# HGRN's last products issued together, two heads per product in MLA and banded attention, and a division one pair behind

## What is computed

```
for l in range(2):
    h = rmsnorm(x)
    a_cq, a_ckv, a_kr, b_q, b_ff, b_fb, b_i, b_g, c_q, c_k, c_v, gates = split(h @ w_in[l])
    y_a = mla(...)      # 8 heads: softmax(q k^T / sqrt(96)) v, q and k of width 96, v of width 64, 512 x 512 scores
    y_b = hgrn2(...)    # ... o = rmsnorm(o_f + o_b, g_out) * silu(g)
    y_c = window(...)   # 8 heads of width 64 that share k and v by fours; blocks of 128 queries see
                        # 3 blocks of keys (2 at the ends); p = exp(s - m) / (sum exp(s - m) + exp(sink - m)),
                        # m = max(max s, sink), s = q k^T / 8 + bias
    x = x + (sum of sigmoid(gate) * (y @ w_br)) @ w_out
    x = x + cross(...);  x = x + swiglu(...)
```

## Time and profile before

| | |
|---|---|
| median of three runs | 4083.86 us |
| profiled execution, its own time / its span | 4075.39 / 4073.2 us |
| busy: PE / DVE / ACT / POOL | 93% / 48% / 37% / 19% |
| mean granted clock of TensorE, in shares of full speed | 0.957 |
| chain that ended last: PE / DVE / ACT / issue / POOL | 75% / 10% / 6% / 5% / 3% |
| MLA's heads, layer 0 and layer 1 (first exponential to last transpose) | 1441.5 to 1511, 2795.9 to 2866 us |
| banded attention, layer 0 and layer 1 (first `ws` to last `ych`) | 1832.9 to 1894.9, 3187.9 to 3251.7 us |

### The profile page before, as it was taken

How to read it: one execution, slowest core, us unless ns; L and a number is a source line. 1 busy time by engine, 2 the same in 40 slices (tenths; PEclk the granted TensorE clock), 3 DMA queues, 4 the chain that set the end, 5 groups by cost and what they waited for, 6 DMA issues and landing times.

```text
span 4073.2 us, 60895 instructions
## 1 busy us (share of the span) xinstructions
PE 3790.8 (93%) x25654; PEld 3075.0 (75%) x25654; DVE 1935.7 (48%) x3078; ACT 1510.6 (37%) x2533; POOL 770.0 (19%) x790
## 2 busy tenths in 40 slices
PE   6889998999999999988999999998999799999998
PEld 3568887887888747776888788875677688777886
DVE  5556555535444565635334533336465533444333
ACT  3433233323323345734223332224575422343222
POOL 0122122221211123432111110102244211101010
PEclk8999999989999899999999999998999899999999
DMA  5321010012222202111223122220111022222222
GB/s 183 125 84 18 3 52 13 3 53 104 99 96 96 68 16 72 59 58 37 97 95 119 59 97 99 97 79 26 62 63 63 16 96 96 88 102 84 98 94 87
DMA packets 81111, 300.87 MB, mean 74 GB/s; under 512 B 8776, under 2 KB 9928, under 8 KB 79944
## 3 DMA queue, kind: packets, MB, share of 16 engines
q1 hardware_dynamic: 80840, 296.99, 21.5%
HBM read 292.76 MB, written 4.19 MB: 73 GB/s over the span
## 4 chain that ended last, share of the span: by engine, by line
PE 75%; DVE 10%; ACT 6%; issue 5%; POOL 3%; DMA 1%; DVEq 0%; SPq 0%; POOLq 0%; ACTq 0%
PE ps L205 74%; PE ps L210 1%; DVE wlo L236 1%; DVE he L244 1%; ACT whi L224 1%; DVE hc L2334 1%; DVE tmp L244 1%; ACT ha L224 1%; DVE ac L244 1%; ACT wp L225 1%; DVE ha L236 1%; ACT L224 1%; DVE ss L244 1%; DVE q L236 1%; DMA wraw<-weights 0%
## 5 line engine op out<-in xcount | busy, mean ns | idle before, releaser
L236 DVE TENSOR_TENSOR wlo<-wraw,whi 128x1024 fp32r<-128x1024 f32 x537 | 682.1, 1275 | 771.6 <-ACT whi L224 770.9
L205 PE MATMUL ps<-hh,whi 128*128 128x512 f32 x1840 | 733.4, 399 | 19.1 <-DVE hl L236 13.9
L205 PE MATMUL ps<-hl,whi 128*128 128x512 f32 x1840 | 723.8, 393 | 0.0
L205 PE MATMUL ps<-hh,wlo 128*128 128x512 f32 x1840 | 723.5, 393 | 0.0
L224 ACT ACTIVATE whi<-wraw 128x1024 fp32r<-128x1024 f32 x537 | 559.8, 1050 | 223.1 <-PE ps L205 169.6
L205 PEld LDWEIGHTS ps<-hh,whi 128*128 128x128 f32 x1840 | 349.8, 190 | 103.7 <-ACT hh L224 20.1
L205 PEld LDWEIGHTS ps<-hh,wlo 128*128 128x128 f32 x1840 | 350.1, 190 | 74.7
L205 PEld LDWEIGHTS ps<-hl,whi 128*128 128x128 f32 x1840 | 350.7, 191 | 70.7
L205 PE MATMUL ps<-u,u 64*64 64x64 f32 (+2 forms) x6016 | 229.0, 228 | 25.6 <-DVE u L236 17.0
L205 PEld LDWEIGHTS ps<-u,u 64*64 64x64 f32 (+1 forms) x6016 | 209.5, 139 | 42.3 <-DVE u L236 18.1
L205 PE MATMUL ps<-gh,whi 128*128 128x512 f32 x528 | 205.4, 389 | 0.0
(11 more groups left out here) (391 smaller groups left out, 7145.7 us busy)
## 6 DMA issues: line engine op xcount, KB each, us to landing
wraw<-weights SPq DMA_DIRECT2D x537, 512.0 KB, 3.2
x<-xT SPq DMA_DIRECT2D x2, 2048.0 KB, 12.4
bias_lines<-ln SPq DMA_DIRECT2D x1, 2048.0 KB
xmf<-memT SPq DMA_DIRECT2D x2, 1024.0 KB, 4.7
out<-x SPq DMA_DIRECT2D x1, 2048.0 KB, 6.2
bias<-bias_lines SPq DMA_DIRECT2D x1, 1536.0 KB, 8.7
con<-consts SPq DMA_DIRECT2D x1, 1378.0 KB, 10.5
ctxt<-ctxT SPq DMA_DIRECT2D x1, 1024.0 KB, 12.5
```

The costliest lines, as they stand in the source:

```text
L205: self.last, self.open = self.e.matmul(out, lhsT, rhs, start=start, stop=stop, skip_group_check=skip), True
L236: return self.e.tensor_tensor(out, a, b, op)
```

## The change

PE, ACT, DVE and POOL get other orders in the two stages; no DMA changes. In short: in MLA PV of two heads is issued after the second head's transposes, the heads in turn for each block of keys, with two buffers `ptt` in place of one, and no bank is held. In HGRN's end POOL does all four `hy` and then all four `hyl`, and ACT does `act_hgrn_out` ahead of the copy `wv`. The banded attention goes by pairs c of heads: the scores of both in turn, then the transposes of pair c-1, head by head, and O of pair c-1, the two heads in turn. DVE adds the bias of one head, divides a head of the pair before, adds the bias of the other head, divides the other one; then it takes all four maxima of a head in one reduce over 4x384 (the two unused ends of 128 are filled with -1e30 once per buffer and layer), with one small operation after it, and at the end of the turn waits for `ych`. `ws` has three buffers.

```diff
-            L.PT = self.ring(f"pt{l}", [self.sb("ptt", M + 4096, [128, 4, 512])], lambda q=qdone: [q()])
+            L.PT = self.ring(f"pt{l}", [self.sb("ptt", M + o, [128, 4, 512]) for o in (4096, 11776)], rdone)
-            L.wS = self.ring(f"ws{l}", [self.sb("ws", M + 3072 + 1536 * i, [128, 4, 384]) for i in range(2)], after_b)
+            L.wS = self.ring(f"ws{l}", [self.sb("ws", M + o, [128, 4, 384]) for o in (3072, 4608, 12288)], after_b)
@@ pe_mla
-                b = ps.take(pe, "mo", l, i // 2, hold=True) if e == 0 else ps["mo", l, i // 2 - 1]
-                q = L.PT[z]
-                for kc in range(4):
-                    hd = i - 1
-                    pe.wait_ge((K.act if kc % 2 else K.dve).at("mt", l, hd, kc), K.act.at("mv", l, 3))
-                    pe.mm(b[64 * e:64 * e + 64, :], L.V[:, kc, hd * 64:hd * 64 + 64], q[:, kc, :], kc == 0, kc == 3)
...
                 if e == 1:
+                    b = ps.take(pe, "mo", l, i // 2 - 1)
+                    for kc in range(4):
+                        pe.wait_ge([(K.act if kc % 2 else K.dve).at("mt", l, hd, kc) for hd in (i - 2, i - 1)], K.act.at("mv", l, 3))
+                        for hd in (i - 2, i - 1):
+                            r, q = slice(64 * (hd % 2), 64 * (hd % 2) + 64), L.PT["ms", l, hd]
+                            pe.mm(b[r, :], L.V[:, kc, hd * 64:hd * 64 + 64], q[:, kc, :], kc == 0, kc == 3)
...
@@ pool_hgrn_out
             pool.tt(s3, L.G4[:, i, :], s2, ALU.mult).then_inc(pool("hy", l, i), 1)
             pool.also(f"ht2{l}", l, i)
+        for i in range(4):
+            s3 = L.t3[l, i]
             pool.wait_ge(K.act.at("hyh", l, i), pool.at("hy", l, i))
             pool.tt(K.Y["b"][1][:, i, :], s3, K.Y["b"][0][:, i, :].bitcast(F32), ALU.subtract).then_inc(pool("hyl", l, i), 1)
@@ pe_window
+        for c in range(5):
+            if c < 4:
+                for n, k0, k1, w, off in K.spans():
+                    b = [ps.take(pe, "ws", l, 2 * c + e, n) for e in range(2)]
+                    pe.wait_ge(act.at("wq", l, c), act.at("wk", l))
+                    for e, r in enumerate(rows):
+                        pe.mm(b[e][:, 0:w], L.wQ[r, c, n * 128:n * 128 + 128], L.wK[r, k0 * 128:k1 * 128])
+                    pe.mark("ws", l, 2 * c + 1, n)
+                    pe.also("ws", l, 2 * c, n)
+            if c > 0:
+                for i in (2 * c - 2, 2 * c - 1):
+                    for n, k0, k1, w, off in K.spans():
+                        b = ps.take(pe, "wt", l, i, n)
+                        pe.wait_ge(K.divided(z, n))
...
+                bo = ps.take(pe, "wo", l, c - 1)
+                for n, k0, k1, w, off in K.spans():
+                    pe.wait_ge([act.at("wt", l, 2 * c - 2 + e, n) for e in range(2)], act.at("wv", l))
+                    for j in range(k1 - k0):
+                        for e, r in enumerate(rows):
+                            q = L.wT["ws", l, 2 * c - 2 + e]
+                            pe.mm(bo[r, n * 128:n * 128 + 128], L.wV[:, k0 + j, 64 * e:64 * e + 64],
+                                  q[:, n, j * 128:j * 128 + 128], j == 0, j == k1 - k0 - 1)
@@ act_window
+        K.act_hgrn_out(l)
         act.wait_ge(pe.at("wv", l))
         act.cp(L.wV.rearrange("p a b -> p (a b)"), ps["wv", l]).then_inc(act("wv", l), 1)
-        K.act_hgrn_out(l)
+        for c in range(5):
+            for i in (2 * c - 2, 2 * c - 1) if c > 0 else ():
+                q = L.wT.take(act, "ws", l, i)
+                for n, k0, k1, w, off in K.spans():
+                    act.wait_ge(pe.at("wt", l, i, n))
+                    act.cp(q[:, n, 0:w], ps["wt", l, i, n][:, 0:w]).then_inc(act("wt", l, i, n), 1)
...
+            for e in range(2) if c < 4 else ():
+                z = ("ws", l, 2 * c + e)
...
                 for n, k0, k1, w, off in K.spans():
                     K.act_exp(z, n, p[:, n, 0:w], s[:, n, 0:w], 1.0)
+                act.also(f"ws{l}", *z)
                 K.act_sink(z, 4, K.vec(f"sink{l}")[:, c + 4 * e:c + 4 * e + 1])
+            if c > 0:
+                act.wait_ge(pe.at("wo", l, c - 1))
+                act.cp(K.Y["c"][0][:, c - 1, :], ps["wo", l, c - 1]).then_inc(act("wo", l, c - 1), 1)
@@ dve_window
+        for s in L.wS.aps:
+            dve.wait_ge(K.ended("hgrn", l))
+            dve.e.memset(s[:, 0:4:3, 256:384], -1e30).then_inc(dve("wpads", l), 1)
+        for c in range(5):
+            for e in range(2):
+                if c < 4:
+                    hd, z = c + 4 * e, ("ws", l, 2 * c + e)
...
+                    for n, k0, k1, w, off in K.spans():
+                        dve.wait_ge(pe.at(*z, n))
+                        dve.stt(s[:, n, 0:w], ps[(*z, n)][:, 0:w], 0.125, ALU.mult, K.bias[:, hd, off:off + w], ALU.add).then_inc(dve("wb", *z), 1)
...
+                if c > 0:
+                    z = ("ws", l, 2 * c - 2 + e)
+                    K.dve_divide(z, [L.wP[z][:, n, 0:w] for n, _, _, w, _ in K.spans()], sink=True)
+            for e in range(2) if c < 4 else ():
+                s, sm = L.wS[z], K.sml.take(dve, *z)
+                dve.e.reduce_max(sm[:, 0:4], s, AXX).then_inc(dve("mx", *z), 1)
+                dve.ts(sm[:, 8:12], sm[:, 0:4], sink, ALU.max, -1.0, ALU.mult).then_inc(dve("ng", *z, 3), 1)
+            if c > 0:
+                dve.wait_ge(act.at("wo", l, c - 1))
+                dve.tt(yl, ps["wo", l, c - 1], yh.bitcast(F32), ALU.subtract).then_inc(dve("wo", l, c - 1), 1)
```

More of the change, by code:

```diff
@@ L2528, in pe_window @@
                 [(b[:, c * 128:c * 128 + 128], c == 0) for c in range(4)], h)
[L2529 to L2532, removed]
+        rows = [slice(64 * e, 64 * e + 64) for e in range(2)]
+        for c in range(5):
+            if c < 4:
                 for n, k0, k1, w, off in K.spans():
-                    b = ps.take(pe, *z, n)
+                    b = [ps.take(pe, "ws", l, 2 * c + e, n) for e in range(2)]
@@ new lines, in pe_window @@
+                    pe.mark("ws", l, 2 * c + 1, n)
+                    pe.also("ws", l, 2 * c, n)
+            if c > 0:
+                for i in (2 * c - 2, 2 * c - 1):
+                    z = ("ws", l, i)
+                    for n, k0, k1, w, off in K.spans():
+                        b = ps.take(pe, "wt", l, i, n)
+                        pe.wait_ge(K.divided(z, n))
+                        for j in range(k1 - k0):
+                            pe.tr(b[:, j * 128:j * 128 + 128], L.wP[z][:, n, j * 128:j * 128 + 128], K.con("id"))
+                        pe.mark("wt", l, i, n)
+                    pe.also(f"wp{l}", *z)
+                bo = ps.take(pe, "wo", l, c - 1)
@@ L2549, in pe_window @@
[L2549 to L2556, removed]
@@ L2576, in act_window @@
         act.also("ps", "wv", l)
-        K.act_hgrn_out(l)
[L2578 to L2581, removed]
-                for n, k0, k1, w, off in K.spans():
[L2583 to L2588, removed]
+        for c in range(5):
+            for i in (2 * c - 2, 2 * c - 1) if c > 0 else ():
+                q = L.wT.take(act, "ws", l, i)
+                for n, k0, k1, w, off in K.spans():
+                    act.wait_ge(pe.at("wt", l, i, n))
+                    act.cp(q[:, n, 0:w], ps["wt", l, i, n][:, 0:w]).then_inc(act("wt", l, i, n), 1)
+                    act.also("ps", "wt", l, i, n)
+            for e in range(2) if c < 4 else ():
+                z = ("ws", l, 2 * c + e)
                 s, p = L.wS[z], L.wP.take(act, *z)
@@ L2591, in act_window @@
                     K.act_exp(z, n, p[:, n, 0:w], s[:, n, 0:w], 1.0)
+                act.also(f"ws{l}", *z)
                 K.act_sink(z, 4, K.vec(f"sink{l}")[:, c + 4 * e:c + 4 * e + 1])
[L2593 to L2596, removed]
+            if c > 0:
+                act.wait_ge(pe.at("wo", l, c - 1))
+                act.cp(K.Y["c"][0][:, c - 1, :], ps["wo", l, c - 1]).then_inc(act("wo", l, c - 1), 1)
+                act.also("ps", "wo", l, c - 1)
         act.mark("end", "window", l)
@@ L2609, in dve_window @@
         K.dve_feed("wv", l)
[L2610 to L2620, removed]
-                sink = K.vec(f"sink{l}")[:, hd:hd + 1]
[L2622 to L2632, removed]
@@ new lines, in dve_window @@
+        for s in L.wS.aps:
+            dve.wait_ge(K.ended("hgrn", l))
+            dve.e.memset(s[:, 0:4:3, 256:384], -1e30).then_inc(dve("wpads", l), 1)
+        for c in range(5):
+            for e in range(2):
+                if c < 4:
+                    hd, z = c + 4 * e, ("ws", l, 2 * c + e)
+                    s = L.wS.take(dve, *z)
+                    dve.wait_ge(K.loaded("bias"))
+                    for n, k0, k1, w, off in K.spans():
+                        dve.wait_ge(pe.at(*z, n))
+                        dve.stt(s[:, n, 0:w], ps[(*z, n)][:, 0:w], 0.125, ALU.mult, K.bias[:, hd, off:off + w], ALU.add).then_inc(dve("wb", *z), 1)
+                        dve.also("ps", *z, n)
+                if c > 0:
+                    z = ("ws", l, 2 * c - 2 + e)
```

(16 more changed lines are left out.)

22 lines of the change are left out of this document (6 added, 16 removed).

## The result

The changed kernel took **4035.27 us**, median of 5 runs (4026.32 to 4047.8); the one before, 5 times in the same session, 4083.86 us (4070.18 to 4100.83). The ratio is 0.9888, 95% interval 0.9848 to 0.9927: 49 us less, where 43 were forecast. In a later session 6 runs of it gave 4046.55 us against 4085.86 (11 runs), ratio 0.9891 (0.9867 to 0.9916).

What follows compares the result with a forecast made beforehand. PE was taken to bound the whole span and MLA, no single engine the banded attention. MLA's -18 and -25 from HGRN's end with the banded attention gave -43 us: 4083.9 to 4041 us, range 4020 to 4066.

Steps and rivals of the forecast that it cites:

- PV by pairs: MLA: two heads' PV on the two column halves takes 3.6 us instead of 7.2; -9.0 us a layer, -18 in all.
- Two middle periods: MLA between head 3 and head 7: a pair takes 14.9 us instead of 17.92; -6.0 us a layer.
- The end: MLA's last head: its transposes have neither scores nor PV for cover while waiting for the division; +1.4 us a layer.
- The start: MLA's start: scores of head 2 begin without PV(0) ahead of them; -4.4 us a layer.
- HGRN's end: POOL's chain finishes ahead of the scores, so DVE's first `ws` starts at 1821.2 instead of 1832.87; -11.7 us a layer.
- Pairs of the banded attention: Turns slightly slower per pair, with DVE waiting for `ych`, yet 60.9 us in sum against 62.0; -1.1 us a layer.
- turn 0: Banded attention's first turn: sums and maxima only, paced by the scores; 7.6 us.
- turn 1: Banded attention's second turn: waits 0.3 us for the sink and meets a slow PE; 15.0 us.
- turn 4: Banded attention's last turn: POOL's division, transposes, copy, then O; 8.1 to 10.2 us, taken as 9.3.
- upper case D: Both stages gain more: POOL's wait hidden in MLA, banded turns of 12.5 us; -62 us, 4022; chance 0.15.
- B: Banded attention: PE's low clock delays transposes and copies, so a turn takes 16.5 us; +12 us, 4053; chance 0.15.
- E: MLA: waits for POOL let PE's clock fall to half; +61 us with the other gain, 4145; chance 0.05.

Runs made afterwards that it cites:

- e3: Changed kernel with a pair's PV in MLA issued one head after the other instead of in turn; MLA 71.7 / 72.3 us in the two layers.
- e2: Kernel before with only the new POOL and ACT orders at HGRN's end; banded attention 105.1 / 105.1 us, profiled run 4065.11 us.
- e9: Kernel before, unchanged, profiled a second time; 4082.24 us, first exponential of MLA at 1451.7 us.
- e5: Changed kernel with ACT copying `ych` between the two new heads' exponentials instead of behind both; banded attention 95.3 / 95.3 us.
- e6: Changed kernel with DVE's `ycl` made one turn later and the products' bank held till then; banded attention 92.8 / 93.1 us.
- e8: Changed kernel with the edits of e6 and e7 together; 4029.39 us median of 6 runs, ratio to the kernel before 0.9871.
- e7: Changed kernel with DVE dividing three of four blocks of every odd MLA head, POOL one instead of two; MLA 63.1 / 63.2 us.
- e11: Changed kernel with the edit of e6, plus DVE's third block for MLA's head 7 alone; 4006.56 us, ratio to before 0.9805.

## Why the prediction was right

**PV by pairs (-18; measured -8.4 and -9.3, -17.7).** The row of HGRN, 16 records in 1.09 us against 20 in 2.40, carried over to 512 columns: 3.65. The Trainium skill, "TensorE: Matmul & The Clock Gate", Part 3, says that a weight load overlaps a matmul in flight only on another row group. The traces contradict it, before the change too: in one head's PV a load at 1461.40 us lies inside the matmul record of 1461.29 to 1461.88 on the same 128 rows. That products on two column halves would bring next to nothing was my inference from it; the same Part lists three tiles side by side in the columns at 2.38 times, and with that these runs agree (two halves, 3.65 us for 7.2). e3 shows that the order of issue is what decides. Two middle periods gave 2 x (17.92 - 14.72) = -6.4, forecast -6.0, since POOL came 0.4 us earlier than I had worked out. The end took 10.9 us from T(6)'s end, forecast 9.3 + 1.4 = 10.7, so it cost 1.6. The start gave -3.7 in layer 0, forecast -4.4: PV(0) is gone from there, but head 2's scores now meet the lower clock in its place, 4.55 us for 3.70.

**HGRN's end (-11.7 a layer; e2: -10.5 and -12.4).** All steps of it stand in the traces: POOL's two lists, ACT's `ybh` ahead of `wv`, the scores as the new releaser. The start of `ws` moved by 12.42 - 0.83 = 11.6 against the scores. That the marks of two layers differ by 2 us belongs to one execution of before: 115.6 and 117.5, in e9 115.5 and 115.9, against which e2 gains 10.4 and 10.8.

**Pairs of the banded attention (-1.1, of which -0.8 was taken; measured -0.8 and -1.0 beyond e2).** The mechanism held: DVE waits for `ych` behind both heads' exponentials. The size did not, and the total hides it. From first `ws` to last `ych`, the mark of the forecast, it is 62.4 us in layer 0 where the sum of turns had 60.9 and before has 62.0: turn 0 7.4 (forecast 7.6), turn 1 15.6 (15.0), then 15.2 and 15.0 (14.5 each), turn 4 9.2 (9.3). Over both profiles of each kernel and both layers it is 62.1 against 62.5 before, 0.5 us less and not 1.1. The longer turns come from T's side: ACT's last `wt` ends at 1857.4, 9.0 after `ycl`'s end at 1848.4, where I had 8.1 for it. About 0.6 of that is the lower clock, 1.97 us for the second head's transposes in place of 1.41, which the forecast of the turn had at nothing. My upper case D took 12.5 for a turn "if ACT takes work before I let it"; e5 shows that it needs an edit, and e6 that 11.35 is there.

**Sum.** -42.4 by the stages, forecast -43. The 4041 us of the forecast lie 6 us over the median of the first session and 6 below that of the second; the runs of one kernel spread over 20 to 30 us, so this is as near as a median of five can tell. No rival came as a whole: PE's clock fell in the banded attention (0.72), where B expected it, and B's mechanism is there, but with some 0.6 us a turn in place of 2.0; in MLA the waits for POOL are 0.23 us and the mean over 1454 to 1520 is 0.90, with the low part at the two ends and PV and scores of the middle pairs at 3.65 and 3.70 as before, so E had nothing to decide on. That the sum came within 1 us is partly luck, since the start of MLA and the turns gave less than forecast, and the middle pairs of MLA and layer 1, long in that one profile of before, gave more.

**What was sized wrong on the way:** e3 at 79 us for 72, because I counted heads in line as wholly serial, though the earlier trace rows had already shown 16 scores in 3.60 against 8 in 2.42, the same effect; e8 at 4005 for 4029, because its base was of another session; and the pair of e7, where I took POOL's wait away and did not ask what DVE's extra block makes late.

## What to carry to other kernels

When an engine stands in line for a result whose producer has other work listed ahead of it, look for the instruction that can be taken a turn later without cost; here that one move (e6) was worth 11 us a layer, as much as the whole reordering of HGRN's end, for one bank held longer. Shift work between engines only where the receiver has slack at that very place: the same third block on DVE cost 0.4 us in a middle pair and gained 2.7 at the end. And compare stages between fixed marks before whole times, since one part that varies by 17 us from execution to execution can hide or double a gain of that size.

## What the runs showed of the hardware

Products of 64 columns of stationary operand on either half of the columns, and products of 64 rows on either half of the rows, run beside each other fully when issued in turn: 16 records of 512 columns in 3.65 us, 16 scores in 2.42, 40 of O in 2.40. Issued in groups they still overlap, by about four records at each change of half: groups of two products lose nothing (3.70), groups of four come to 5.42. I had expected neither the overlap in line nor its limit.

Over the 62 us from the first `ws` of the banded attention on, the granted clock fell from 0.87 (before, 1833 to 1895 us) to 0.72 (changed, 1826 to 1888), with PE's busy time per us down from 0.79 to 0.68. It cost little, about half a us a turn: in two turns of e5 that follow each other eight transposes take 1.97 and 1.41 us, and the turns 12.53 and 12.09. With DVE's wait gone (e11, 1805 to 1856 us) it was 0.87 again.
